# Gate and up products of six feed-forward networks by Strassen's seven block products, in a three-layer float32 transformer on Trainium2

## The reference, cut to what matters

```python
D_MODEL, SEQ, N_META, D_FF = 1024, 512, 16, 2816

def _swiglu(x, wi, wo):
    a, b = jnp.split(x @ wi, 2, axis=-1)      # wi: 1024 x 5632, wo: 2816 x 1024
    return (jax.nn.silu(a) * b) @ wo

for layer in range(DEPTH):                    # first block: DEPTH = 2, 528 tokens
    h = h + 0.5 * _swiglu(_rms_norm(h, ln_ffn1[layer]), ffn1_wi[layer], ffn1_wo[layer])
    h = h + mix @ w_out[layer]                # two kinds of attention
    h = h + 0.5 * _swiglu(_rms_norm(h, ln_ffn2[layer]), ffn2_wi[layer], ffn2_wo[layer])
# second block: one layer over the last 512 tokens, with a state-space scan, a dilated
# and a memory attention between its two networks, then a final norm
```

## Time and profile before

| | |
|---|---|
| median of 3 runs | 3736.02 us (3735.87 to 3737.22) |
| the profiled execution | 3736.37 us, of which the span from the first to the last instruction is 3734.7 us |
| PE busy | 3566.8 us, 96% of the span |
| DVE busy | 1741.1 us, 47% |
| ACT busy | 1300.1 us, 35% |
| POOL busy | 440.0 us, 12% |
| mean granted clock of TensorE | 0.976 |

### The profile page before, as it was taken

How to read it: one execution, slowest core, us unless ns; L and a number is a source line. 1 busy time by engine, 2 the same in 40 slices (tenths; PEclk the granted TensorE clock), 3 DMA queues, 4 the chain that set the end, 5 groups by cost and what they waited for, 6 DMA issues and landing times. The chain is left out here.

```text
span 3734.7 us, 50566 instructions
## 1 busy us (share of the span) xinstructions
PE 3566.8 (96%) x20104; PEld 2920.9 (78%) x20104; DVE 1741.1 (47%) x2492; ACT 1300.1 (35%) x1793; POOL 440.0 (12%) x465
## 2 busy tenths in 40 slices
PE   8999799799999999989999999999999899799998
PEld 7999777699999999755547888888744477678886
DVE  5442466544434443266625443443377533545433
ACT  4332266433323332134525432342110243324421
POOL 0000222100000000010006400000144233220000
PEclk9999899899999999989999999999999999999999
DMA  4322311022222222300013222222212421233222
GB/s 168 135 88 85 122 55 51 18 91 90 83 85 102 90 86 78 136 26 23 1 34 113 101 88 103 101 90 90 101 51 85 120 78 51 107 108 108 94 85 84
DMA packets 116172, 318.07 MB, mean 85 GB/s; under 512 B 13815, under 2 KB 56951, under 8 KB 100052
## 3 DMA queue, kind: packets, MB, share of 16 engines
q1 hardware_dynamic: 116052, 316.51, 25.0%
HBM read 307.98 MB, written 17.01 MB: 87 GB/s over the span
## 5 line engine op out<-in xcount | busy, mean ns | idle before, releaser
L332 PE MATMUL acc<-fb_xh,fb_wh 128*128 128x264 f32 x1408 | 287.8, 286 | 5.5 <-DVE fb_wl L489 5.5
L332 PE MATMUL acc<-fb_xl,fb_wh 128*128 128x264 f32 x1408 | 288.1, 286 | 0.0
L332 PE MATMUL acc<-fb_xh,fb_wl 128*128 128x264 f32 x1408 | 287.7, 286 | 0.0
L332 PE MATMUL acc<-fd_xh,fd_wh 128*128 128x512 f32 x704 | 275.6, 391 | 5.5 <-DVE fd_wl L489 5.5
L332 PE MATMUL acc<-fd_xl,fd_wh 128*128 128x512 f32 x704 | 274.6, 390 | 0.0
L332 PE MATMUL acc<-fd_xh,fd_wl 128*128 128x512 f32 x704 | 274.6, 390 | 0.0
L332 PEld LDWEIGHTS acc<-fb_xh,fb_wh 128*128 128x128 f32 x1408 | 220.1, 189 | 5.8 <-DVE fb_wl L489 5.7
L407 ACT ACTIVATE fb_wh<-fb_raw 128x2048 fp32r<-128x2048 f32 (+1 forms) x74 | 124.7, 1686 | 286.9 <-PE acc L391 173.8
L332 PEld LDWEIGHTS acc<-fb_xl,fb_wh 128*128 128x128 f32 x1408 | 219.3, 189 | 0.0
L332 PEld LDWEIGHTS acc<-fb_xh,fb_wl 128*128 128x128 f32 x1408 | 219.0, 189 | 0.0
L484 DVE TENSOR_TENSOR fb_wl<-fb_raw,fb_wh 128x2048 fp32r<-128x2048 f32 (+1 forms) x74 | 148.3, 2004 | 141.5 <-ACT fb_wh L407 140.6
(11 more groups left out here) (532 smaller groups left out, 8766.0 us busy)
## 6 DMA issues: line engine op xcount, KB each, us to landing
fb_raw<-wi_dram SPq DMA_DIRECT2D x42, 1024.0 KB, 4.8
fd_raw<-wi_dram SPq DMA_DIRECT2D x42, 1024.0 KB, 4.8
fb_raw<-wo_dram SPq DMA_DIRECT2D x32, 704.0 KB, 4.0
fd_raw<-wo_dram SPq DMA_DIRECT2D x32, 704.0 KB, 4.0
fa_raw<-wi_dram SPq DMA_DIRECT2D x20, 1024.0 KB, 4.8
ff_raw<-wi_dram SPq DMA_DIRECT2D x20, 1024.0 KB, 4.8
a_raw<-a_qkv_dram SPq DMA_DIRECT2D x24, 512.0 KB, 4.2
s_gw<-gate_w_dram SPq DMA_DIRECT2D x24, 512.0 KB, 3.8
```

Of the source, the lines that this page charges most:

```text
L332: last = pe.matmul(acc[:, up_base(p, b) + 2 * a + q, 0:w], x[:, k, a, :], part[:, k, t0:t0 + w], start=k == 0 and part is xh and x is wv, ...
```

## The change

The inner part of `ffn_stage` is written anew for every network. The two networks' shapes, the weights' layout in memory and the loaded bytes stay.

*Seven products.* In chunks 2 to 21, the pair (gate, up) by (input chunks 0 to 3, 4 to 7) by (first half of the tokens, second half) is a two-by-two block product, made as seven products (the Winograd form of Strassen's algorithm). Each has 4·3 matmuls of 264 or 256 columns and its own bank. Seven weight operands are rounded and split (512 elements per partition each) in place of four such quarters: three are sums made by GpSimd, and a fourth sum is written over a raw block. Seven state operands are made once per network (`sums_of_x`, on GpSimd). Chunks 0 and 1 stay plain, with 96 matmuls of half width.

*A ring.* Rounded and split weights go through a ring of 8 entries; at step x ScalarE waits until product x is made and rounds entry x + 8. Raw weights have 3 slots. Entries 1, 2 and 4 of a chunk, all of the second product and the first plain chunk are split by GpSimd, the others by VectorE.

*Groups.* The second product runs in four groups of hidden chunks (0 to 5, 6 to 10, 11 to 16, 17 to 21), each over 8 output chunks, two up chunks behind the first product. So stretches of seven-product chunks are 6, 5, 6 and 3 long. `gh` and `gl` have 8 slots in place of 22. `h` is added to four times per output chunk.

*Start of a network.* The square root now comes, in ScalarE's order, after the operands of the state and four roundings. All loops are unrolled.

*Rotation tables.* They are made on GpSimd in `dsa_stage`, in a free part of `mix`, stored to memory before the third output weight is loaded, and loaded again in `scan_stage`. ScalarE's store of head 10 waits for that.

```diff
+            w, HK, RING, LEAD, RAW, SLOTS_ = n // 2, KC // 2, 8, 2, 3, 8
...
+            DOWN = ((0, 6), (6, HF), (HF, HF + 6), (HF + 6, FC))
...
+            for d, (u0, u1) in enumerate(DOWN):
+                made_up = sum(kind == "up" for kind, _, _ in jobs)
+                jobs += [("up", u, 0) for u in range(made_up, min(u1 + 2, FC))]
+                jobs += [("dn", d, c) for c in range(KC)]
...
+            PLAIN, SEVEN = (A11, A21, A12, A22), (1, 6, 5, 2, 3, 7, 4)
...
+            def by_pool(i, p):
+                return i == 0 or (i > 1 and p in (1, 2, 4, D0_, D1_))
...
+                        def weight_sums(net, i, p):
...
+                            if p == 6:
+                                raw_landed(pool, net, i, 1)
+                                last_read(net, i, 5)
+                                pool.tensor_tensor(s1, a21, a22, ALU.add).then_inc(sums, 1)
+                                last_read(net, i, 6)
+                                pool.drain()
+                                pool.tensor_tensor(s2, s1, a11, ALU.subtract).then_inc(sums, 1)
+                            elif p == 3:
+                                last_read(net, i, 3)
+                                pool.drain()
+                                pool.tensor_tensor(s4, a12, s2, ALU.subtract).then_inc(sums, 1)
+                            elif p == 7:
+                                pool.tensor_tensor(a21, a11, a21, ALU.subtract).then_inc(sums, 1)
...
+                        for p in PLAIN:
+                            rest_of_weights(0, 0, p)
+                        for net in range(NETS):
+                            for k in range(HK):
+                                sums_of_x(net, k)
+                            pool.wait_ge(t_lo, 1 + HK * (net + 1))
+                            for i, p in order[RING:RING + LEAD]:
+                                weight_sums(net, i, p)
+                            for x in range(PER):
+                                if x + RING + LEAD < PER:
+                                    weight_sums(net, *order[x + RING + LEAD])
+                                e = PER * net + x + RING
+                                if e < PER * NETS and by_pool(*order[e % PER]):
+                                    rest_of_weights(e // PER, *order[e % PER])
...
+                        def product(net, i, p):
+                            bank_wait(pe, net, i, p)
+                            lo_wait(pe, net, i, p)
+                            if i == 2 and p == 6:
+                                pe.wait_ge(t_lo, 1 + HK * (net + 1))
+                            for m in range(HK):
+                                ms = slice(m * P, (m + 1) * P)
+                                for x, part in ((wh, xh), (wh, xl), (wl, xh)):
+                                    last = pe.matmul(acc[:, bank(net, i, p), 0:w], entry(x, net, i, p)[:, ms],
+                                                     part[:, X_PART[p], m, :], start=m == 0 and x is wh and part is xh,
+                                                     stop=m == HK - 1 and x is wl)
+                            last.then_inc(made, 1)
...
+                            for x, (i, p) in enumerate(order):
...
+                                if p == 1:
+                                    copy_first(net, i)
+                                if i > 1 and p in (1, D0_) and jobs[i - 1][0] == "up":
+                                    round_hidden(net, jobs[i - 1][1])
+                                e = PER * net + x + RING
+                                if e < PER * NETS:
+                                    round_weights(e // PER, *order[e % PER])
+                                if x == 3:
+                                    act.wait_ge(summed, 1 + net + 1)
+                                    act.activation(folded(rstd[:, :], n), acc[:, bank(net, 1, A12):
+                                                                              bank(net, 1, A12) + np_, 0:wide], ACT.Sqrt,
+                                                   scale=1.0 / D, bias=eps_t[:, :]).then_inc(rooted, 1)
+                                    silu(net, 0)
+                                    round_hidden(net, 0)
...
+                                elif p == 7:
+                                    silu(net, i)
...
+                        def seven_out(net, i, p):
+                            of = acc[:, bank(net, i, p), 0:w]
+                            dve.wait_ge(made, made_by(net, i, p))
+                            if p == 6:
+                                dve.wait_ge(copied, 1 + of_act * net + jobs[i][1] - 1)
+                                dve.tensor_tensor(u2, of, x1, ALU.add).then_inc(outs, 1)
+                                dve.drain()
+                            elif p == 5:
+                                dve.tensor_tensor(u4, of, u2, ALU.add).then_inc(outs, 1)
+                                dve.drain()
+                            elif p == 2:
+                                dve.tensor_tensor(gate[:, 0:w], of, x1, ALU.add).then_inc(outs, 1)
+                                dve.drain()
+                            elif p == 3:
+                                dve.tensor_tensor(gate[:, w:n], of, u4, ALU.add).then_inc(outs, 1)
+                                dve.drain()
+                                dve.tensor_tensor(gate[:, :], gate[:, :], rstd[:, :], ALU.mult).then_inc(gated, 1)
+                            elif p == 7:
+                                dve.tensor_tensor(u3, of, u2, ALU.add)
+                                dve.tensor_tensor(up[:, w:n], of, u4, ALU.add).then_inc(outs, 1)
+                                dve.drain()
+                            elif p == 4:
+                                dve.tensor_tensor(up[:, 0:w], of, u3, ALU.add).then_inc(outs, 1)
+                                dve.drain()
+                                dve.tensor_tensor(up[:, :], up[:, :], rstd[:, :], ALU.mult)
+                                dve.drain()
+                                hidden(net, jobs[i][1])
...
-                    arm(pool, "fd_", "t_")
+                    arm(pool, "fd_")
+                    tables.work(pool)
...
+                        if hd == 10:
+                            act.wait_ge(tables.stored, 49)
```

983 lines of the change are left out of this document (562 added, 421 removed).

## The result

The changed kernel takes 3897.6 us (median of 4 runs, 3897.3 to 3900.8) against 3736.4 before: ratio 1.0433, 95% interval 1.0415 to 1.0451. It is 161 us slower. The profiled execution lasted 3897.3 us with a span of 3895.6.

The account below looks back on a forecast made before the run. TensorE, busy for 96% of the span, was taken as the bound, so only fewer columns would help. 3736.4 - 132 + 200 + 82 + 6 + 5 = 3897 us; own range 3800 to 3990, stated range 3740 to 4010.

Parts of the forecast that it names:

- Columns: TensorE in the feed-forward networks: 84 matmuls in place of 96 per seven-product chunk, -132 us in all.
- Waits in stretches: TensorE waiting for splits in runs of seven-product chunks: 33 us per network, +200 us over six.
- T: Time VectorE and GpSimd need per steady seven-product chunk: 14.4 us, lower end 13.3 (4.4 + 8.9), upper end 16.
- the formula: Wait of an n-chunk stretch: 7n - 8 heavy steps, each (T - 10.1)/7 too slow, less 10.1 us of ring cover.
- so the lead is won back: Between stretches, GpSimd's two splits (some 2 us) lie beside 4.1 us of TensorE, so the ring's cover refills.
- The mechanism: In steady chunks, VectorE's 8 two-SBUF operations and GpSimd's 7 exclude each other: 5.5 + 8.9 = 14.4 us.
- Starts: Start of each network: the root queues behind state and weight sums and TensorE waits, +61 and +21, together +82 us.
- The last group: End of each network: hidden split read after 2.7 us but ready after about 3.7, +1 per network, +6 us.
- Tables: Rotation tables made on GpSimd in 138.5 us, ending after head 10's store: +5 us (0 to +15).
- No exclusion: Rival for the stretches: GpSimd's splits slip between VectorE's, 0 in place of +200, 3697 us; chance 0.12.
- Short holds: Rival for the stretches: GpSimd's hold is shorter than its duration, T = 12.3, waits 38 us, 3735 us; chance 0.10.
- Half clock in stretches: Rival for the waiting stretches: T = 16, or half clock with 2.56 us per 256-column product, near 4033 us; chance 0.10.

Follow-up runs that it names:

- runs 3: Changed kernel with GpSimd's weight splits and sums replaced by zero fills that read nothing, so results lack those parts: 3713.3 us.
- run 4: Changed kernel with VectorE's four splits per seven-product chunk left out, so the result lacks a correction term: 3730.8 us, ratio 0.9988.
- run 2: Changed kernel with three splits of each seven-product chunk (entries 1, 2, 4) moved from GpSimd to VectorE: 3979.2 us, ratio 1.0651.
- run 5: Changed kernel with one more split of each seven-product chunk (entry 7) moved from VectorE to GpSimd: 3926.2 us, ratio 1.0511.
- run 1: Changed kernel with ScalarE's square root issued during the rounding of the state sums, not behind them: 3875.3 us, ratio 1.0377.
- run 10: Changed kernel with single seven-product chunks among down chunks, four plain chunks, state sums behind the root, three of four parts behind the fourth chunk's weights: 3792.1 us.

## Why the prediction was right

The total came out within 1 us, which is luck of size: the sum of the terms' errors is near zero.

- **Columns**, -132 forecast, -138 measured. The spacing of 256 columns was exact (0.120); at 264 it is 0.1212, and not the 0.1224 that the first product had in the kernel before. Its second product stood at 0.1211 there already (1056 matmuls in 127.9 us).
- **Waits in stretches**, +200 forecast, +153 measured: the term that was oversized. T was put at 14.4, each VectorE operation counted at its full 0.69; it is 13.3. At T = 13.3 the formula gives 10.6, 2.2 and 5.4 us for the three stretches that wait (18.4 per network, +110). The 512-token networks have 11.3, 3.5 and 10.6. So the first stretch was understood, but the step "so the lead is won back" failed: behind the second down group, which lasts 27.2 us, a stretch of six waits 5 us more than a full lead allows. In the 528-token networks that group lasts 29.2 us and the same stretch waits 7.4 to 8.7; behind the first group, 32.7 us long, the lead was nearly full. The forecast's second six was right by two errors (10.8, 10.6).
- **The mechanism**, exclusion of operations with two SBUF operands, was right and is shown by runs 3 and 4. As a sum it was not complete, and that 4.4 + 8.9 gives just the measured 13.3 is chance. GpSimd's hold is some 1.15 us and not 1.27, as the rows of the steady chunk show. With 0.55 and 1.15 the turns add up to 12.4 us for the change, 10.2 for run 4, 10.6 for run 2 and 13.0 for run 5, where 13.3, 10.8, 14.6 and 13.4 were measured. In run 2 VectorE's own queue is the bound. In the others 0.4 to 0.9 us are left over, and in the change VectorE idles 1.22 us a chunk for ScalarE's rounding; how much of the rest that link makes is not separated by any run. The prediction had named this link (ScalarE rounds nothing for the next chunk until the silu product is done) and gave it no price.
- **Starts**, +82 forecast; +106 inside the networks, and most of the +11 outside. The chain was followed rightly (from TensorE's first matmul to the first product a stage's first network takes 19.1 to 21.0 us longer, forecast 12.9, and its first matmul stands 7.5 us behind ScalarE's first operation, forecast 6.9; a second network takes 12.9 and 15.2 us longer, forecast 10.4). Missed: squares that wait for VectorE's additions, up to 2.6 us, so that the first pair was ready at 15.3 and not 12.5; and the first state part, which takes 11.2 us because its operands stand behind ScalarE's roundings and VectorE's four splits (the other three take 4.6, 4.6 and 3.1). The root came at 44.6 and not 37.9. That the root's place is the cause was assumed in the sum and is a third right (run 1).
- **The last group**, +6 forecast, +26 measured. The step that failed is "about 3.7 us" for the last chunk's tail against 2.7 of cover: the rows below show 0.86, 1.05, the rounding at 2398.32 and the split to 2399.67, behind a VectorE that ends the chunk's additions late: 5.7 us from the last product's end, not 3.7. TensorE's and VectorE's timeline of the changed kernel:

```profile
2399.73 0.50 PE L565 MATMUL acc<-fd_gh,fd_wh 128*128 128x512 f32 x1 [2.98 <-DVE fd_gl L742]
```

```profile
2396.30 0.86 DVE L778 TENSOR_TENSOR fd_up<-fd_up,fd_rstd 128x512 f32<-128x512 f32 x1
2397.23 1.05 DVE L737 TENSOR_TENSOR fd_up<-fd_up,fd_gate 128x512 f32<-128x512 f32 x1
2398.98 0.69 DVE L742 TENSOR_TENSOR fd_gl<-fd_up,fd_gh 128x512 fp32r<-128x512 f32 x1 [0.70 <-ACT fd_gh L639]
```

- **Tables**, +5 forecast, 0 measured: GpSimd makes them in 114 us, not 138, and the store had no wait.
- **Rivals.** No exclusion (3697 us) fell: with GpSimd reading, T is 13.3; the run without its reads came to 3713 us. Short holds (T = 12.3, 3735 us) fell in its time and not in its premise: GpSimd's hold is shorter than its duration, but the two queues do not pack to it. Half clock in stretches fell but for one stretch of eighteen (0.94 in the first network's five, 1.00 in the others); the starts ran at 0.76 to 0.86. The price of T = 16 is +330 by the formula and not +336, which changes nothing; and 3990 as the upper end of the forecast's own range leaves that T out, since with it the sum is near 4030.
- The signs named ahead held: six pauses before the root (10.8 to 12.5 us, named as 8 to 11), stretches of three without waiting, additions from the accumulator at 0.43 us, the two-SBUF operations well over 0.69. A chunk near a stretch's end takes 13.3 us, not 14.

Open stays how much of the starts' cost could be removed. In run 10 the starts are some 68 of 106 us shorter, but its first stretch, of three chunks, waits 5.3 us in every network, 32 together. It has more plain chunks and several changes of order at once, and the part of each was not separated further. Open too is whether a change of ScalarE's order alone would bring the 13.3 us down.

## What to carry to other kernels

Before taking products from TensorE, add up what the engines that feed it must do per saved product, with operations that exclude one another counted as one queue, each engine's own queue apart, and every wait for a third engine whose order ties the two together: here 1.6 or 0.8 us of columns per chunk were bought with 3.2 us of lag. A cover of a few entries lends time and does not make it; it is won back only where those engines really idle, and as fully as that time is long (27.2 us were too short here, 32.7 nearly enough). Work moved into that time can cost the stretch behind it. Price the start of a stage by following the chain of every engine to the first matmul of the new kind, for moving one link (the root) moved the wait and kept two thirds of it.

## What was not expected of the hardware

- A VectorE operation with two SBUF operands that meets a reading GpSimd operation ends 0.54 to 0.55 us behind that one's end (128 x 512), whether it began 0.5 or 1.1 us before; alone it takes 0.69. The other way round GpSimd's operation ends 1.13 to 1.17 us behind VectorE's; alone it takes 1.26 to 1.29. A GpSimd fill of the same tile left it at 0.692 in mean of 120.
- GpSimd's subtraction of 128 x 512 takes 1.26 to 1.29 us alone and 1.52 in mean of the 128 splits of a stage; as two instructions of half the columns it takes 1.9 in the steady chunk.
- Matmuls of 264 columns stood 0.1212 us apart (252 in 30.54 us), against 0.1224 in the first product before and 0.1211 in its second product. Why is open.
